# A two-layer hybrid backbone on one core: constant loads and a gate's modulation moved at the start, output chunks moved into the last attention stage

## The chip, the cores and the metric

One core of a Trainium2 chip runs the whole program. TensorE (PE) multiplies matrices out of SBUF into PSUM; its clock is granted at one of two levels, 1.2 and 2.4 GHz, which the profile gives as a share (0.50 and 1.00). VectorE (DVE), ScalarE (ACT) and GpSimd (POOL) do element-wise work; SyncE (SP) and ACT issue DMAs, each on a queue of its own (q1 is SP's, q10 is ACT's), and both queues feed the same 16 DMA engines. The metric is the device time of one execution in microseconds; the median of the timed runs counts, and less is better.

## The reference, cut to what matters

```python
D_MODEL, SEQ, CTX_LEN, DEPTH, D_FF = 1024, 512, 256, 2, 2816

for i in range(DEPTH):                      # layer 0: pooling mixer, layer 1: differential attention
    mod_l = (silu(c) @ ada_w[i] + ada_b[i]).reshape(9, D_MODEL)      # latent: shift, scale, gate for 3 sub-layers
    mod_c = (silu(c_ctx) @ ada_w[i] + ada_b[i]).reshape(9, D_MODEL)  # the same for the context tokens
    x = x + 0.5 * md[2] * swiglu(rms_norm(x) * g * (1 + md[1]) + md[0])          # first half step
    x = x + md[5] * mixer(rms_norm(x) * g * (1 + md[4]) + md[3])
    x = x + 0.5 * md[8] * swiglu(rms_norm(x) * g * (1 + md[7]) + md[6])          # second half step

# the attention of layer 1, for each of 8 heads
p = softmax(q @ k.T / 8)                    # twice, on two halves of the head
a = p[0] - lam * p[1]
o = rms_norm(a @ v, sub_g) * (1 - lam_init) # then o @ w_o, over all heads
```

Everything is float32. The 512 latent tokens and the 256 context tokens go through together; in layer 1 only the latent ones are kept after the attention.

## The kernel before, in words

Activations lie transposed: a tile holds 128 features by 768 tokens, and there are 8 such tiles. Every large product is taken in three passes on values split in a high and a low part (`h_hi`, `h_lo` and `w_hi`, `w_lo`): high times high, high times low, low times high. Per 128 output features (a *unit*; two units, `ch` 0 and 1, make a *pair*) ACT writes `w_hi` (L777), DVE writes `w_lo` (L1797), and PE multiplies (`chunk`, L1250, one chunk for one of the 8 feature tiles). The order on every engine is written out by hand in five programs, one for each engine, which meet in semaphores; nothing is scheduled by a tool. Each engine runs its instructions in that order, so whatever stands behind a waiting instruction waits too.

**The start.** SP issues the tokens (`xstage`), group 0 of the first modulation (`first_raw`, L526, 2 MB: shift and scale for two feature tiles, from `ada_w`), the weights of unit pair 0, and groups 1 to 3. ACT's queue brings the small tables, among them seven DMAs for constants that are used much later: `edge_sb` (pooling), `rope_sb`, four parts of `gqk` and `lam_sb` (attention), 576 KB in all. PE transposes the tokens (L1754), multiplies group 0 by silu(c) (`first_products`, L1492), spreads the inverse norm (L1482), multiplies group 1, and then alternates: the two feature tiles of a group through pair 0 for both `ch` (`first_pair`), then the products of the group after next. DVE turns a group's products into the modulation and makes `h_lo` (L2106).

**The modulation of the rest.** The first half step needs its gate (numbers 16 to 23 of the 72 blocks of 128 features) only where its first output pairs add to `x`. Two of these blocks come by a DMA of 1 MB (`gate_raw`, L564) and 32 small matmuls with two columns each (`gate_products`, L1504), which stand behind pair 1. The others come in *granules* of three blocks: SP loads 1.5 MB in two halves (`ada_raw`, L534), DVE multiplies and adds (L1814), ACT and POOL split the sum (L784, L790, L705), and two pairs later PE reduces it (`reduce_granule`, L1326, 18 matmuls with one column). One granule goes beside one pair of the FFN: 18 in the first FFN, beside pairs 1 to 18 of 30. The gate is made after pair 10 (`add_bias(0, GATE_FIRST, ...)`).

**The last attention stage.** The attention runs head by head; in stage `h` PE projects head `h`, scores head `h-1` over four tiles `s` of 128 queries (`score`, L1574), transposes its weights one tile behind (`turn_weights`, L1584), and head `h-2` gets its norm (`out_sums` L1611, `out_spread` L1622; DVE `out_norm` L2264). In the last stage (`h` = 8) nothing is left to project, and the product with `w_o` begins: `out_chunk(j)` is head `j`'s part of the first two output units, three matmuls of 512 columns for each `ch`, in bank `pv`. It needs ACT's `out_hi(j)` (L1138) and DVE's `out_lo(j)` (L2268). Chunks 0 and 1 stand in tile 0, chunk 2 behind the tiles, and chunks 3 to 7 after `values` (L1593, the product of weights and values), among the steps of the last head's norm. Then `unit` multiplies the other output pairs (bank `pu`).

## Time and profile before

| | us |
|---|---|
| three runs, median (lowest to highest) | 2584.11 (2583.5 to 2585.42) |
| the profiled execution | 2582.41 |
| its span (first to last instruction) | 2580.5 |
| PE busy | 2502.1 (97%) |
| DVE busy | 1564.8 (61%) |
| ACT busy | 872.6 (34%) |
| POOL busy | 427.4 (17%) |

A busy PE means that a matmul was in flight; at half the clock the same matmul is busy for longer, so the busy time says nothing of the clock. The granted clock is 0.98 over the whole span. All times of rows are from the span's start.

### The profile page before, as it was taken

What the parts mean: (1) busy time and instruction counts of PE and PEld (TensorE: products, weight loads), DVE (VectorE), ACT (ScalarE), POOL (GpSimd) and SP (SyncE); (2) the same over time, 40 slices, a digit from 0 to 9 for tenths busy, and PEclk for the clock granted to TensorE, in tenths of its full rate; (3) what the DMA queues carried; (4) which work ended last, traced back from release to release, by engine and by line L of the source; (5) the groups of instructions that cost most, each with busy time, mean ns of one, the idle gap of its engine ahead of it and who ended that gap; (6) DMA issues with size and microseconds to landing.
All of it is one profiled execution on the core that took longest, in us unless ns stands there. A gap on an engine that the chain in (4) does not pass through costs nothing.

```text
span 2580.5 us, 40749 instructions
## 1 busy us (share of the span) xinstructions
PE 2502.1 (97%) x14775; PEld 2217.2 (86%) x14775; DVE 1564.8 (61%) x2442; ACT 872.6 (34%) x1360; POOL 427.4 (17%) x517
## 2 busy tenths in 40 slices
PE   7999999999899999999999999999899988999999
PEld 7888888888788888888789999998789977788887
DVE  3788675224688857882584757574777774433332
ACT  2333132213533323331242423243455553322221
POOL 0121111001212111120100000001477751000000
PEclk9999999999899999999999999999899999899999
DMA  7555443221155534542122212222110111233332
GB/s 224 151 150 155 146 118 94 63 73 44 30 151 161 156 114 136 159 133 67 33 66 59 80 57 75 64 65 66 49 50 25 48 33 50 78 98 94 97 101 87
DMA packets 367021, 238.76 MB, mean 93 GB/s; under 512 B 7681, under 2 KB 365666, under 8 KB 366946
## 3 DMA queue, kind: packets, MB, share of 16 engines
q1 hardware_dynamic: 365104, 237.01, 31.4%
q10 hardware_dynamic: 1842, 0.77, 0.1%
q8 instruction: 45, 0.74, 0.1%
q14 instruction: 30, 0.25, 0.0%
HBM read 235.65 MB, written 2.10 MB: 92 GB/s over the span
## 4 chain that ended last, share of the span: by engine, by line
PE 91%; DVE 4%; ACT 2%; issue 1%; DMA 1%; POOL 1%; SPq 0%; ACTq 0%; DVEq 0%; POOLq 0%
PE pu L1250 63%; PE pu L1404 11%; PE pv L1556 5%; PE pu L1258 3%; PE pv L1492 1%; PE pu L1574 1%; PE pv L1584 1%; PE pu L1593 1%; DMA first_raw<-in_ada_w 1%; DVE h_lo L2106 1%; PE pv L1326 1%; DVE xn L2099 1%; PE pu L1529 1%; PE pu L1682 1%; DVE w_lo L1797 1%
## 5 line engine op out<-in xcount | busy, mean ns | idle before, releaser
L1250 PE MATMUL pu<-h_hi,w_hi 128*128 128x512 f32 (+1 forms) x1808 | 515.5, 350 | 3.4 <-DVE w_lo L1797 3.2
L1250 PE MATMUL pu<-h_hi,w_lo 128*128 128x512 f32 (+1 forms) x1808 | 513.5, 348 | 0.0
L1250 PE MATMUL pu<-h_lo,w_hi 128*128 128x512 f32 (+1 forms) x1808 | 513.2, 348 | 0.0
L1797 DVE TENSOR_TENSOR w_lo<-w_raw,w_hi 128x1024 fp32r<-128x1024 f32 (+3 forms) x228 | 311.3, 1366 | 249.8 <-ACT w_hi L777 242.3
L777 ACT ACTIVATE w_hi<-w_raw 128x1024 fp32r<-128x1024 f32 (+3 forms) x228 | 247.6, 1087 | 568.6 <-PE pu L1250 512.9
L1814 DVE SCALAR_TENSOR_TENSOR ada_acc<-ada_raw,cs,ada_acc 128x384 f32<-128x384 f32 x588 | 337.3, 616 | 10.7 <-DVE ada_acc L1814 1.8
L1250 PEld LDWEIGHTS pu<-h_hi,w_hi 128*128 128x128 f32 x1808 | 289.3, 188 | 50.7 <-DVE w_lo L1797 4.0
L1250 PEld LDWEIGHTS pu<-h_hi,w_lo 128*128 128x128 f32 x1808 | 289.9, 188 | 45.8
L1250 PEld LDWEIGHTS pu<-h_lo,w_hi 128*128 128x128 f32 x1808 | 289.0, 188 | 45.4
L2025 DVE SCALAR_TENSOR_TENSOR xT<-pu,gate,xT 128x512 f32 (+3 forms) x136 | 81.3, 634 | 332.1 <-PE pu L1250 329.0
L705 POOL TENSOR_TENSOR ada_acc<-ada_acc,ada_parts 128x768 f32<-128x768 f32 x84 | 142.3, 1694 | 726.8 <-ACT ada_parts L784 686.4
L1250 PE MATMUL pu<-a_hi,w_hi 128*128 128x512 f32 (+1 forms) x792 | 227.4, 350 | 0.6
L1250 PE MATMUL pu<-a_hi,w_lo 128*128 128x512 f32 (+1 forms) x792 | 226.4, 349 | 0.0
L1250 PE MATMUL pu<-a_lo,w_hi 128*128 128x512 f32 (+1 forms) x792 | 226.4, 349 | 0.0
L1250 PEld LDWEIGHTS pu<-a_hi,w_hi 128*128 128x128 f32 x792 | 127.2, 188 | 21.3 <-issue 0.4
L1250 PEld LDWEIGHTS pu<-a_hi,w_lo 128*128 128x128 f32 x792 | 127.1, 188 | 20.9
L1250 PEld LDWEIGHTS pu<-a_lo,w_hi 128*128 128x128 f32 x792 | 127.1, 188 | 20.8
L784 ACT ACTIVATE ada_parts<-ada_acc 128x768 bf16<-128x768 f32 x42 | 35.5, 845 | 322.0 <-PE pv L1326 310.2
L2011 DVE TENSOR_TENSOR prod<-pu,sil 128x512 f32<-128x512 f32 x116 | 63.3, 580 | 120.0 <-PE pu L1250 115.9
L801 ACT ACTIVATE sil<-pu 128x512 f32<-128x512 f32 x116 | 54.1, 508 | 222.7 <-PE pu L1250 222.7
L653 POOL TENSOR_TENSOR sqa<-sq 128x768 f32<-128x768 f32 (+2 forms) x6 | 9.1, 1517 | 666.4 <-ACT sq L822 659.5
L1556 PE MATMUL pv<-w_hi,h_hi 128*128 128x384 f32 (+1 forms) x336 | 112.4, 334 | 4.5 <-DVE w_lo L2254 4.5
(267 smaller groups left out, 4430.9 us busy)
## 6 DMA issues: line engine op xcount, KB each, us to landing
w_raw<-in_ffn_w_in SPq DMA_DIRECT2D x138, 512.0 KB, 3.9
ada_raw<-in_ada_w SPq DMA_DIRECT2D x84, 768.0 KB, 4.7
w_raw<-in_ffn_w_out SPq DMA_DIRECT2D x48, 704.0 KB, 4.6
w_raw<-in_ffn_w_in SPq DMA_DIRECT2D x76, 256.0 KB, 3.0
w_raw<-in_diff_w_qkv SPq DMA_DIRECT2D x24, 512.0 KB, 5.4
first_raw<-in_ada_w SPq DMA_DIRECT2D x8, 1024.0 KB, 12.2
w_raw<-in_ffn_w_out SPq DMA_DIRECT2D x16, 384.0 KB, 3.5
w_raw<-in_ffn_w_out SPq DMA_DIRECT2D x16, 320.0 KB, 3.2
```

The lines of the kernel that those rows point to most:

```text
L705: nc.gpsimd.tensor_tensor(rest, rest, ada_parts[:, i, :], ALU.subtract).then_inc(rest_ready, 1)
L777: act.activation(w_hi[:, ch, 0:k * P], w_raw[:, ch, 0:k * P], ACT.Copy).then_inc(hi_ready[ch], 1)
L784: act.activation(ada_parts[:, 0, :], ada_acc[:].rearrange("p s n -> p (s n)"), ACT.Copy).then_inc(part_ready, 1)
L801: i = act.activation(sil[:, SEG[s]], ps(0, s), ACT.Silu)
L1250: last = pe.matmul(banks(ch, s_), w[:, j, :], r[:, SEG[s_]], start=(j == 0 and i == 0), stop=(j == k - 1 and i == 2))
L1258: last = pe.matmul(tail_bank(i_, ch, s_), w[:, j, :], r[:, j, seg(i_, s_)], start=(j == 0 and i == 0), stop=(j == k - 1 and i == 2))
L1404: last = pe.matmul(pu[:, bank_of[p], 0:HN], w_[:, j, :], x_[:, j, :], start=(not adds and j == 0 and i == 0), stop=(j == HK - 1 and i == 2 ...
L1556: last = pe.matmul(pv[:, t % 2, at:3 * DV], x_[:, j, t * P:(t + 1) * P], aw[w_][:, j, at:], start=(j == 0 and i == 0), stop=(j == DC - 1 a ...
L1797: dve.tensor_tensor(w_lo[:, ch, 0:k * P], w_raw[:, ch, 0:k * P], w_hi[:, ch, 0:k * P].bitcast(F32), ALU.subtract).then_inc(split_ready[ch], 1)
L1814: last = dve.scalar_tensor_tensor(ada_acc[:, s_, :], ada_raw[:, b, i, :], w, ada_acc[:, s_, :], ALU.mult, ALU.add)
L2011: last = dve.tensor_tensor(prod[:, SEG[s]], ps(1, s), sil[:, SEG[s]], ALU.mult)
L2025: last = dve.scalar_tensor_tensor(xT[:, m, SEG[s]], banks(ch, s), gate[:, gk, s, m], xT[:, m, SEG[s]], ALU.mult, ALU.add)
```

## The change

It has three parts at the start and two in the last attention stage.

1. The seven constant DMAs go from ACT's program to SP's, behind group 3 of the first modulation.
2. `gate_raw`, its DMA and `gate_products` are gone. Granules begin one earlier (`ADA_FIRST` 5 for 6), so the first FFN has 19, beside pairs 1 to 19; the first of them holds blocks 15 to 17 (15 is computed once more and not used). Pair 1 on PE moves from a place of its own into the loop.
3. In `first_pair` the last group runs both its feature tiles for `ch` 0 and then both for `ch` 1, where before `ch` alternated within each tile.
4. Chunks 2, 3 and 4 stand behind the transposes of tiles 0, 1 and 2, chunk 5 where chunk 2 was, and the ACT and DVE parts that feed them move ahead accordingly. After `values` come chunk 6 for `ch` 0, the sums, the spread, chunk 7 for `ch` 0, then 6 and 7 for `ch` 1.
5. For the last head ACT squares straight from PSUM, before it copies to `oT`, where before it copied first and squared the copy. DVE's norm waits for that copy.

```diff
-ADA_FIRST = 2 * DC // ADA_CH + 1
+ADA_FIRST = 2 * DC // ADA_CH
-GATE_CH = ADA_CH * ADA_FIRST - GATE_FIRST
@@ SP
                         sp.wait_ge(h_ready[1], DC * (2 * n + 1))
-                        if n == 0:
-                            sp.dma_start(gate_raw[:], first[:, :, 2, 0:GATE_CH * P]).then_inc(gate_in, 16)
                         load_granule(n, 0)
...
             load_first(3)
+            sp.dma_start(edge_sb[:], edge.rearrange("g s e -> (g s e)").partition_broadcast(P)
+                          .rearrange("p (g s e) -> p g s e", g=len(WINDOWS), s=4)).then_inc(in_par2, 16)
+            sp.dma_start(rope_sb[:], rope.rearrange("t p a d -> p t a d")).then_inc(in_par2, 16)
+            for i in range(4):
+                sp.dma_start(gqk[:, i, :], qk_g[0, i // 2].partition_broadcast(P)).then_inc(in_par2, 16)
+            sp.dma_start(lam_sb[:], lam_p[0].rearrange("a d -> (a d)").partition_broadcast(P)
+                          .rearrange("p (a d) -> p a d", a=4)).then_inc(in_par2, 16)
             load_ffn(0)
@@ ACT, attn_act
+                if not do_a:
+                    out_hi(2)
                 for s in range(TT):
...
-                    if not do_a and s < QT:
-                        out_hi(s + 2)
+                    if not do_a and s < QT - 1:
+                        out_hi(s + 3)
...
                 if not do_a:
                     out_hi(HEADS - 2)
+                    act.wait_ge(pv_done, HEADS)
+                    act.wait_ge(ors_done, HEADS)
+                    act.activation(ob[:], pu[:, 0, :], ACT.Square).then_inc(osq_ready, 1)
@@ ACT, the seven constant loads go from here, and out_square(HEADS - 1) from behind attn_act(HEADS, ...)
...
@@ PE, ffn_pe
                             first_pair()
-                            for ch in range(2):
-                                unit(ch, 1, DC, lambda j: h_hi[:, j], lambda j: h_lo[:, j], n)
-                            gate_products()
-                            first = 2
+                        first = 1
@@ PE, first_pair
                 for g in range(GROUPS):
-                    for j in (2 * g, 2 * g + 1):
+                    js = (2 * g, 2 * g + 1)
+                    for j, ch in [(j, ch) for j in js for ch in range(2)] if g < GROUPS - 1 else [(j, ch) for ch in range(2) for j in js]:
@@ PE, attn_pe
                     if do_b and 1 <= s <= QT:
                         turn_weights(g, s - 1)
+                    if not do_a and 1 <= s < QT:
+                        out_chunk(s + 1)
...
-                    out_chunk(2)
+                    out_chunk(QT + 1)
                     out_spread(h - 2)
@@ PE, behind attn_pe(HEADS, ...)
-            out_chunk(3)
+            out_chunk(HEADS - 2, (0,))
             out_sums(HEADS - 1)
-            out_chunk(4)
             out_spread(HEADS - 1)
-            for j in range(5, HEADS):
-                out_chunk(j)
+            out_chunk(HEADS - 1, (0,))
+            for j in (HEADS - 2, HEADS - 1):
+                out_chunk(j, (1,))
@@ DVE, attn_dve
-                        out_lo(2)
+                        out_lo(QT + 1)
                     if do_b and 1 <= s <= QT:
                         weights_lo(g, s - 1)
+                    if not do_a and s < QT - 1:
+                        out_lo(s + 2)
                     if do_b and s < QT:
                         combine(step, g, s)
@@ DVE, behind attn_dve(HEADS, ...)
-            for j in range(3, HEADS - 1):
-                out_lo(j)
+            out_lo(HEADS - 2)
             out_var(HEADS - 1)
+            dve.wait_ge(oT_ready, HEADS + 1)
             out_norm(HEADS - 1)
```

What this makes of each engine's order, at three places (the third for PE and for ACT). Line numbers differ between the two kernels, since the change adds and removes lines.

SP's program at the start (the DMAs in the order in which they are issued), before:

```order
L526 DMA first_raw<-in_ada_w 128x8x256 [waits x_squares,xt_done]
L526 DMA first_raw<-in_ada_w 128x8x256 x3
L539 DMA w_raw<-in_ffn_w_in 128x8x128 [waits split_ready0]
L539 DMA w_raw<-in_ffn_w_in 128x8x128 [waits split_ready1]
L564 DMA gate_raw<-in_ada_w 128x8x256 [waits h_ready1]
L534 DMA ada_raw<-in_ada_w 128x4x384 [waits ada_half0]
L534 DMA ada_raw<-in_ada_w 128x4x384 [waits ada_half1]
```

and after:

```order
L520 DMA first_raw<-in_ada_w 128x8x256 [waits x_squares,xt_done]
L520 DMA first_raw<-in_ada_w 128x8x256 x3
L574 DMA edge_sb<-in_edge 128x128
L576 DMA rope_sb<-in_rope 128x4x128
L578 DMA gqk<-in_diff_qk_g 128x64 x4
L579 DMA lam_sb<-in_diff_lambda 128x256
L533 DMA w_raw<-in_ffn_w_in 128x8x128 [waits split_ready0]
L533 DMA w_raw<-in_ffn_w_in 128x8x128 [waits split_ready1]
L528 DMA ada_raw<-in_ada_w 128x4x384 [waits ada_half0,h_ready1]
L528 DMA ada_raw<-in_ada_w 128x4x384 [waits ada_half1]
```

The seven constant DMAs stand between group 3 and the weights of pair 1, and the gate's DMA is gone from behind them.

PE's program in the last attention stage, from the end of one tile's scores (`kT`, `qT`) over the transposes of the tile before (`ident,a`) to the next tile's scores, before:

```order
L1574 MATMUL pu<-kT_hi,qT_lo 128x384 x2
L1584 MATMUL pv<-ident,a 128x128 x6
L1574 MATMUL pu<-kT_hi,qT_hi 128x384 x2
L1574 MATMUL pu<-kT_lo,qT_hi 128x384 x2
L1574 MATMUL pu<-kT_hi,qT_lo 128x384 x2
```

and after (`h`, `w` are the operands of a chunk):

```order
L1557 MATMUL pu<-kT_hi,qT_lo 128x384 x2
L1567 MATMUL pv<-ident,a 128x128 x6
L1246 MATMUL pv<-h_hi,w_hi 128x512
L1246 MATMUL pv<-h_lo,w_hi 128x512
L1246 MATMUL pv<-h_hi,w_lo 128x512
L1246 MATMUL pv<-h_hi,w_hi 128x512
L1246 MATMUL pv<-h_lo,w_hi 128x512
L1246 MATMUL pv<-h_hi,w_lo 128x512
L1557 MATMUL pu<-kT_hi,qT_hi 128x384 x2
```

One chunk, six matmuls, has come between the transposes and the next scores.

PE's program behind the last head's `values`, from its sums of squares (`ones,ob`) on, before:

```order
L1611 MATMUL pu<-ones,ob 128x1 x4
L1250 MATMUL pv<-h_hi,w_hi 128x512
L1250 MATMUL pv<-h_lo,w_hi 128x512
L1250 MATMUL pv<-h_hi,w_lo 128x512
L1250 MATMUL pv<-h_hi,w_hi 128x512
L1250 MATMUL pv<-h_lo,w_hi 128x512
L1250 MATMUL pv<-h_hi,w_lo 128x512
L1622 MATMUL pu<-ident,orms 128x128 x4
L1250 MATMUL pv<-h_hi,w_hi 128x512
```

and after:

```order
L1594 MATMUL pu<-ones,ob 128x1 x4
L1605 MATMUL pu<-ident,orms 128x128 x4
L1246 MATMUL pv<-h_hi,w_hi 128x512
L1246 MATMUL pv<-h_lo,w_hi 128x512
L1246 MATMUL pv<-h_hi,w_lo 128x512
L1246 MATMUL pv<-h_hi,w_hi 128x512
```

No chunk stands between the sums and the spread any more. On ACT the square of the last head comes ahead of the copy; before:

```order
L1123 ACTIVATE aT_hi<-pv 128x3x128 [waits ta_done] x2
L1138 ACTIVATE h_hi<-oT 128x512 [waits on_ready]
L1170 ACTIVATE oT<-pu 128x512 [waits pv_done]
L1134 ACTIVATE ob<-oT 128x512 [waits ors_done,oT_ready]
L1138 ACTIVATE h_hi<-oT 128x512 [waits on_ready]
```

and after:

```order
L1122 ACTIVATE aT_hi<-pv 128x3x128 [waits ta_done] x2
L1137 ACTIVATE h_hi<-oT 128x512 [waits on_ready]
L1171 ACTIVATE ob<-pu 128x512 [waits ors_done,pv_done]
L1174 ACTIVATE oT<-pu 128x512 [waits pv_done]
L1137 ACTIVATE h_hi<-oT 128x512 [waits on_ready]
```

The square no longer waits for the copy, and the copy stands behind it.

## Rows read from the trace of the kernel before

**Rows 1.** The page: the chain that ended last, by engine.

```profile
PE 91%; DVE 4%; ACT 2%; issue 1%; DMA 1%; POOL 1%; SPq 0%; ACTq 0%; DVEq 0%; POOLq 0%
```

**Rows 2.** Waits of PE: who for whom, us in total, times, longest.

```profile
PE pu L1574 <- ACT e L1116: 11.0, 4, 4.3
```

**Rows 3.** Timeline of PE, first 131 us: start, us, instruction [idle before <-releaser].

```profile
24.53 8.71 PE L1492 MATMUL pv<-cs,first_raw 128*128 128x128 f32 x64 [3.10 <-DMA first_raw<-in_ada_w]
...
34.42 7.31 PE L1492 MATMUL pv<-cs,first_raw 128*128 128x128 f32 x64
...
57.05 7.31 PE L1492 MATMUL pv<-cs,first_raw 128*128 128x128 f32 x64
...
74.13 0.61 PE L1250 MATMUL pu<-h_hi,w_hi 128*128 128x512 f32 x2 [1.45 <-DVE w_lo L1797]
...
130.39 0.60 PE L1326 MATMUL pv<-ones_bf,ada_parts 128*128 128x1 bf16 x18
```

**Rows 4.** The chain of waits, first 100 us: start, us, what.

```profile
74.13 16.91 PE pu L1250 x96
91.05 3.47 PE pv L1504 x32
```

**Rows 5.** DMA queues from 8 to 24.5 us: packets, MB, share of 16 engines.

```profile
q10 hardware_dynamic: 1534, 0.64, 16.4%
```

**Rows 6.** DMA issues at 24.2 and 40 us (median us to landing); SP's timeline.

```profile
first_raw<-in_ada_w SPq DMA_DIRECT2D x2, 1024.0 KB, 9.6
...
40.04 3.39 SPq L539 DMA_DIRECT2D w_raw<-in_ffn_w_in  x1
...
w_raw<-in_ffn_w_in SPq DMA_DIRECT2D x1, 512.0 KB, 9.9
```

**Rows 7.** Timelines of DVE and ACT, first 110 us.

```profile
66.97 2.20 DVE L2106 SCALAR_TENSOR_TENSOR h_lo<-xn,mod,h_hi 128x512 fp32r<-128x512 f32 x4
...
71.76 1.06 ACT L777 ACTIVATE w_hi<-w_raw 128x1024 fp32r<-128x1024 f32 x1 [3.94 <-PE pu L1250]
```

**Rows 8.** Windows: us; busy of PE, PEld, DVE, ACT, POOL; PEclk, DMA, GB/s.

```profile
23.90:27.30 3.40, 2.77 (x13) 2.80 (x14) 0.00 (x0) 1.06 (x1) 0.00 (x0) 0.50 0.90 272
95.60:99.00 3.40, 3.40 (x12) 2.86 (x11) 3.12 (x6) 0.84 (x1) 0.05 (x1) 0.50 0.91 220
113.00:130.40 17.40, 17.35 (x109) 14.91 (x105) 15.09 (x21) 6.04 (x8) 3.33 (x2) 1.00 0.52 151
2119.70:2133.30 13.60, 8.30 (x40) 6.68 (x41) 11.07 (x22) 6.53 (x14) 0.00 (x0) 0.50 0.01 1
```

**Rows 9.** Timeline of PE in and behind the last attention stage.

```profile
2124.11 0.69 PE L1574 MATMUL pu<-kT_hi,qT_hi 64*128 64x384 f32 x2 [2.43 <-ACT e L1116]
...
2126.33 1.54 PE L1584 MATMUL pv<-ident,a 128*128 128x128 f32 x6
...
2149.39 1.05 PE L1611 MATMUL pu<-ones,ob 128*128 128x1 f32 x8
...
2151.78 1.16 PE L1622 MATMUL pu<-ident,orms 128*128 128x128 f32 x8
...
2158.82 0.50 PE L1250 MATMUL pu<-h_hi,w_hi 128*128 128x512 f32 x1 [1.79 <-DVE w_lo L1797]
```

**Rows 10.** The chain of waits in the same stretch.

```profile
2139.80 2.56 PE pv L1250 x6
2142.35 1.54 PE pu L1622 x8
...
2148.04 1.40 PE pv L1250 x6
```

**Rows 11.** Timelines of DVE and ACT in the same stretch.

```profile
2130.19 0.17 DVE L2242 RECIPROCAL rz<-zz 128x2 f32<-128x2 f32 x1 [0.59 <-ACT e L1116]
...
2154.42 0.69 DVE L2268 TENSOR_TENSOR h_lo<-oT,h_hi 128x512 fp32r<-128x512 f32 x1 [0.70 <-ACT h_hi L1138]
...
2148.70 0.63 ACT L1134 ACTIVATE ob<-oT 128x512 f32<-128x512 f32 x1
```

More of the change, by code:

```diff
@@ L1496, in first_products @@
                 last.then_inc(first_done, 1)
-            def gate_products():
-                pe.wait_ge(gate_in, 16)
-                for c_ in range(GATE_CH):
-                    at = 2 * (GATE_FIRST + c_)
-                    for j in range(DC):
-                        pe.matmul(pv[:, 2, at:at + 2], gate_raw[:, j, c_ * P:(c_ + 1) * P], cs[:, j::DC],
-                                  start=(j == 0), stop=(j == DC - 1))
             def first_pair():
@@ L1624, in out_spread, with out_chunk @@
                 last.then_inc(ors_done, 1)
-            def out_chunk(j):
+            def out_chunk(j, chs=(0, 1)):
                 if j == 0:
@@ L1632, in out_chunk @@
                 pe.wait_ge(on_split, j + 1)
-                for ch in range(2):
+                for ch in chs:
                     last = chunk(ch, j, DC, h_hi[:, j], h_lo[:, j], NL, wo_banks)
```

21 lines of the change are left out of this document (3 added, 18 removed).

## The prediction, made before the changed kernel was run

> **What bounds the kernel now.** I read the page's chain first: 91% of it is PE [rows 1], so the kernel is bound by PE's own matmuls, and only two kinds of thing can change the time by much: work that leaves PE, and the few places where PE waits or runs at 1.2 GHz. PE's waits are short and I looked for those at the change's places. At the start PE is free at 24.53 - 3.10 = 21.43 and waits 3.10 us for the DMA of group 0 [rows 3]. It waits 1.45 us for the split weights of pair 1 at 74.13 [rows 3]. In the attention it waits for ACT's exponentials, 11.0 us in 4 waits [rows 2], three of which lie in the last stage, the one shown 2.43 us long [rows 9]. Behind that stage it waits 1.79 us at 2158.82 for split weights [rows 9]. The windows show where the clock is at the lower of its two levels: 23.9 to 27.3 right after the 3.1 us wait, 95.6 to 99.0 right after the gate's small products, and 2119.7 to 2133.3 in the last attention stage [rows 8].
>
> **The constant loads.** From 8 to 24.5 us ACT's queue takes 16.4% of the 16 engines [rows 5], that is 0.164 x 16.5 = 2.7 us of all of them, and nearly all of its 0.64 MB is the seven moved DMAs (0.58 MB). Without them everything on SP's queue can land up to 2.7 us sooner: group 0 at about 21.8 and not 24.4. PE is free at 21.43, so its wait shrinks from 3.1 to some 0.4 us. The first products took 8.71 us, the later ones 7.31 [rows 3], and their first 3.4 us were at level 0.50 [rows 8]; with so short a wait I expect the full level, 1.4 us less. PE would be ready for group 1's products at 34.42 - 2.7 - 1.4 = 30.3. But group 1's second half is issued at about 24.2 and lands 9.6 us later, at 33.8 [rows 6], so this DMA comes next: 33.8 - 2.7 = 31.1. Start of the second products 34.42 -> 31.2: **-3.2**. From there the chain at the start is PE's own. Bounds: -1.5 (the queue keeps its own pace and only part of the share is returned, the clock still falls but for less) and -4.3 (PE itself is the limit: 34.42 - 30.1). The loads land later on SP's queue instead; pair 1's second weights are issued at 40.04 and landed at 49.9 [rows 6], ACT wants them at 71.76 [rows 7], so 2.7 us more there, and 3 us for seven issues, lie within 21 us of slack: 0.
>
> **The order in first_pair.** 96 matmuls take 16.91 us [rows 4], so two feature tiles for two units, 24 matmuls, take 4.2 and one tile for one unit 1.05. Before, unit 0 ended one such piece ahead of unit 1; now two. ACT's `w_hi` at 71.76 and DVE's `w_lo` behind it come 1.05 sooner, and PE's wait goes from 1.45 to 0.4: **-1.05**. What may take this back: tile 7 is needed sooner. Its `h_lo` ends at 66.97 + 2.20 = 69.17 [rows 7]; PE's last products start at 57.05 and take 7.1 of their 7.31 us before the next starts, two tiles follow (4.2), so PE comes to tile 7 of unit 0 at 68.3 + 1.05 = 69.4. That fits by 0.2. Bounds 0 and -1.45.
>
> **The gate.** The 32 small products go: **-3.5** [rows 4]. Pair 2's weights were split before they ended, so pair 2 follows at once. The stretch at level 0.50 behind them holds 12 matmuls in 3.4 us [rows 8] where full level gives twice as many: it cost about 1.6 us. I think the light products caused it, because dense pairs lie before and after and no wait: **-1.6**, bounds 0 and -1.7. One granule more is 18 matmuls on PE, **+0.6** [rows 3]. Beside a pair with a granule, DVE is busy 15.1 of 17.4 us, ACT 6.0 and POOL 3.3 [rows 8], so one more such pair is hidden on all three; it falls on pair 19, far from the end of that FFN at 30, and the gate still takes nine reduced granules by pair 10: 0. If DVE were not to fit, each microsecond over 17.4 would be one on PE. Dropping 1 MB from SP's queue ahead of granule 0 and adding 1.5 MB in the middle is hidden (DMA share 0.52 there).
>
> The Trainium skill (TensorE: Matmul & The Clock Gate, Part 1: The HAM clock gate) speaks against counting on the clock: it says that the slow stretch at the ramp varies from run to run with the same kernel, and that one should not fit to a count of slow matmuls. By that rule the terms for the clock would be left out and the start would give some 2 to 3 us less. The trace has both stretches only once, so it can't refute it.
>
> Start together: -3.2 - 1.05 - 3.5 - 1.6 + 0.6 = **-8.8**.
>
> **The tiles of the last stage.** A tile takes PE 2.2 us for scores (2124.11 to 2126.33), then the transposes [rows 9], then it waits about 2.4 us for the next exponentials. A chunk takes 1.40 us at full clock and 2.56 at half [rows 10]. So three of the four chunks go into waits that exist: at half clock they would overrun by 0.1 us at most. DVE waits 0.59 us for the exponentials [rows 11], and one `out_lo` (0.69) is put there: 0.1 us. What PE does more keeps it from light stretches, so the clock should come back earlier than 2133.3. Where it does, tiles shrink by a few tenths, and transposes, chunk and spread behind the last tile, which took 1.2 + 2.56 + 1.54 = 5.3 us at half clock [rows 9, 10], take 3.2. Bounds +0.4 (no better clock, small overruns) and -2.9. I take **-1.7**.
>
> **Behind the tiles.** Let V be the end of `values`, 2148.04 [rows 10]; the next unit starts at 2158.82, V+10.8. Now: ACT's square comes 0.63 sooner [rows 11], so the sums start at V+0.75 (2149.39 - 0.63). From sums to spread it took 2149.39 to 2151.78 [rows 9], 2.4 us, with a chunk as cover that is now gone: spread at V+3.15. From the spread's start to the end of the last `h_lo` it took 2151.78 to 2155.11 [rows 9, 11], 3.3 us: V+6.5. Chunk 7 of unit 0, half of 1.40: V+7.2. Then ACT's and DVE's split of the next weights, 2.4 us from ACT's start to PE's (71.76 to 74.13 [rows 3, 7], the same two steps): the unit starts at V+9.65, **-1.15**. But PE now idles 1.4 + 2.3 + 1.05 us of these 9.65, and the clock fell after stretches with such waits at 23.9 and at 2119.7 [rows 8]. Then spread and chunk are slower (1.54 for 1.0, 1.28 for 0.7 [rows 10]), which brings V+10.8 back, and the unit starts at half clock: 1.7 us lost if that goes on for as long as the shortest stretch of rows 8. Bounds -1.15 and +2.5. With some of both I take **0**.
>
> **Sum:** -8.8 - 1.7 + 0 = -10.5 us. It is made against the profiled execution (span 2580.5, time 2582.41), which lies 1.7 below the median of the three runs; taken to the median, 2584.1 - 10.5 = **2573.6**.
>
> **Rivals.**
> - *No head start.* Group 0 isn't held by the small loads but by SP's own 2 MB and the pace of its queue. For it: SP's own bytes before group 1 are ten times as many. Against: both share the engines and 16.4% is measured. Then 3.2 less of the gain: -7.3, 2576.8. The Trainium skill (DMA: Bandwidth & Descriptors, Issuing engines are not separate DMA queues) says that the engines interleave what any issuer started and that issuing from another one saves only the time to issue; by it the move of queue gives nothing, only the move behind the groups does. The trace agrees in that q10 took 16.4% of the engines beside SP's queue [rows 5].
> - *The tail gives it back.* The two bare waits behind the sums and the spread put the clock at half, the tiles gain nothing: -8.8 + 2.5 = -6.3, 2577.8. For it: the windows of 2119.7 to 2133.3. Against: chunks keep PE busier before it.
> - *Everything holds.* Group 1 doesn't bind (-4.3), all of the 1.45 goes, full clock in the tiles (-2.9) and behind (-1.15): about -13.7, 2570.4.
> - *Slower.* SP's program is in order and the weights of pair 1 and granule 0 now stand behind seven DMAs. If each had to land before the next is issued, at the 9.6 us of rows 6, 7 x 9.6 = 67 us would pass; from 21.8 us on (71.76 - 49.9) PE waits, so 45 us lost against 10.5 won: 2618. Against: SP was done with one issue in 3.39 us where its transfer took 9.9 to land [rows 6], so issues overlap.
>
> **Chances.** Forecast 0.55, no head start 0.17, tail gives back 0.15, everything holds 0.10, slower 0.03. A change of 0.2% (5.2 us) is about what the runs can tell from none. The first four are all beyond it, but both the second and the third together give -3.1, so I put 0.09 on within it: faster 0.88, same 0.09, slower 0.03. Range 2570.3 to 2578.3: it takes in both smaller gains and the full one, and leaves out their combination and the slower case.
>
> **What would show it.** The wait at the first group is under 1 us and the window behind it is at level 1.00; the second products start near 31; the wait for pair 1's weights is 0.4; no `gate_raw`, and no half-clock stretch near 90; PE's row for the granules has 774 matmuls for 756. In the last stage a chunk stands in each of three tiles with the wait for ACT shrunk by it; behind `values` two idle gaps of 1.4 and 2.3 us that name POOL or DVE. Wrong would be: a second group that lands at 33.8 as before, PE waiting for DVE beside pair 19, or a tile period that grows beyond 6.2 us (2124.11 to 2130.3).

## The result, and the profile after

The changed kernel takes 2570.57 us (median of 5 runs, 2568.22 to 2574.07), the kernel before 2584.33 in the same measurement (5 runs, 2583.5 to 2586.32). The ratio is 0.9941, 95% interval 0.9929 to 0.9953, that is 12.1 to 18.3 us less. A second measurement of both gave 2572.56 (5 runs) against 2586.92 (23 runs), ratio 0.994, interval 0.9927 to 0.9953. Forecast were 10.5 us less and 2573.6. The direction was right, the gain that was forecast was too small by 3 to 5 us. The median of 2570.57 lies at the lower edge of the stated range (2570.3 to 2578.3); the ratio, taken to the 2584.11 of before, gives 2568.9, which is below it.

The profiled execution took 2570.57 us with a span of 2568.8. PE is still the bound; the chain of the page now reads:

```profile
PE 90%; DVE 5%; ACT 2%; issue 2%; POOL 1%; DMA 1%; SPq 0%; ACTq 0%; DVEq 0%; POOLq 0%
```

**The start.** The timeline of PE in the changed kernel, to be held against [rows 3]:

```profile
20.30 7.31 PE L1484 MATMUL pv<-cs,first_raw 128*128 128x128 f32 x64
...
28.93 7.42 PE L1484 MATMUL pv<-cs,first_raw 128*128 128x128 f32 x64
...
67.71 0.62 PE L1246 MATMUL pu<-h_hi,w_hi 128*128 128x512 f32 x2 [0.41 <-DVE w_lo L1782]
...
101.74 0.60 PE L1322 MATMUL pv<-ones_bf,ada_parts 128*128 128x1 bf16 x18
```

The first products wait for nothing and run at full clock (7.31 us where they took 8.71); the second ones start at 28.93 and not at 34.42, 5.5 us sooner where 3.2 were forecast. The wait for pair 1's weights is 0.41 us, as forecast. The reduction of the first granule starts at 101.74; before, it started at 112.67. The chain of waits says what holds group 0. Before (start, us, what):

```profile
4.34 20.06 DMA first_raw<-in_ada_w
...
24.53 8.71 PE pv L1492 x64
```

and after:

```profile
3.44 8.70 DMA xstage<-in_ctx
...
19.37 0.87 PE pu L1739 x6
20.25 0.22 PE pv L1743 x2
20.46 7.15 PE pv L1484 x64
```

Before, the last link was the group's own DMA, 20 us long. Now the last DMA on the chain is the one of the context tokens, which lands at 12.1; from there PE's and DVE's transposes run without a gap. Group 0 itself is no longer on the chain. How long its two halves take from issue to landing, first before (the second half is issued at 4.34 and lands at 24.4) and then after (it is issued at 4.4 and lands at 18.2):

```profile
DMA to landing us min/median/max: 15.0/17.5/20.1
```

```profile
DMA to landing us min/median/max: 11.2/12.5/13.8
```

So group 0 lands 6.2 us sooner where 2.7 were forecast, ahead of the end of the transposes, and PE's own work sets the start of its products. The queues from 8 to 24.5 us, first before (packets, MB, mean rate; then the share of q1, SP's queue; q10 is in [rows 5]):

```profile
DMA packets 5451, 4.62 MB, mean 280 GB/s; under 512 B 765, under 2 KB 5180, under 8 KB 5451
...
q1 hardware_dynamic: 3917, 3.98, 73.5%
```

and after:

```profile
DMA packets 5914, 5.63 MB, mean 341 GB/s; under 512 B 172, under 2 KB 5638, under 8 KB 5914
...
q1 hardware_dynamic: 5771, 5.58, 108.9%
```

Taking 16.4% of the engines away from q10 gave q1 35 points more, and all queues together 61 GB/s more. The moved loads had cost more than the share that they took. The share adds up the times of the packets; since it can reach 108.9%, it isn't a part of a fixed 100% of which one queue gets what another leaves.

**The gate.** Behind pair 1 there is no half-clock stretch any more. Windows of the changed kernel (us; busy of PE, PEld, DVE, ACT, POOL; granted clock, DMA share, GB/s), against the second row of [rows 8]:

```profile
88.00:92.00 4.00, 4.00 (x25) 3.48 (x24) 3.76 (x5) 0.84 (x1) 1.43 (x1) 1.00 1.12 296
92.00:96.00 4.00, 4.00 (x25) 3.44 (x24) 3.37 (x6) 1.82 (x3) 0.00 (x0) 1.00 0.02 5
```

From pair 1 to the first reduced granule it takes 34.03 us, where it took 38.54.

**The last stage.** The timeline of PE, against [rows 9]:

```profile
2107.25 0.45 PE L1557 MATMUL pu<-kT_hi,qT_hi 64*128 64x384 f32 x2 [1.76 <-ACT e L1115]
...
2113.24 0.44 PE L1557 MATMUL pu<-kT_hi,qT_hi 64*128 64x384 f32 x2 [0.64 <-ACT e L1115]
...
2118.61 0.45 PE L1557 MATMUL pu<-kT_hi,qT_hi 64*128 64x384 f32 x2 [1.10 <-ACT e L1115]
...
2124.35 1.03 PE L1594 MATMUL pu<-ones,ob 128*128 128x1 f32 x8 [1.10 <-ACT e L1115]
...
2136.99 1.05 PE L1594 MATMUL pu<-ones,ob 128*128 128x1 f32 x8
2139.38 1.16 PE L1605 MATMUL pu<-ident,orms 128*128 128x128 f32 x8 [1.34 <-POOL orms L746]
...
2142.84 0.80 PE L1246 MATMUL pv<-h_hi,w_hi 128*128 128x512 f32 x1 [2.30 <-DVE h_lo L2253]
...
2146.95 0.50 PE L1246 MATMUL pu<-h_hi,w_hi 128*128 128x512 f32 x1 [0.46 <-DVE w_lo L1782]
```

The same waits in the kernel before, besides the one of 2.43 us at 2124.11 that [rows 9] show:

```profile
2118.12 0.44 PE L1574 MATMUL pu<-kT_hi,qT_hi 64*128 64x384 f32 x2 [1.78 <-ACT e L1116]
...
2130.30 0.69 PE L1574 MATMUL pu<-kT_hi,qT_hi 64*128 64x384 f32 x2 [2.44 <-ACT e L1116]
...
2136.24 1.36 PE L1611 MATMUL pu<-ones,ob 128*128 128x1 f32 x8 [2.46 <-ACT e L1116]
```

The three waits for ACT behind a chunk shrank from 2.4 us to 0.64, 1.10 and 1.10, and a tile takes 5.99, 5.37 and 5.74 us (2107.25 to 2113.24, 2118.61, 2124.35) where it took 5.99, 6.19 and 5.94 (2118.12 to 2124.11, 2130.30, 2136.24): 1.0 us less in all. Behind `values` stand the forecast waits that name POOL and DVE, 1.34 and 2.30 us. The clock of this stretch, against the last row of [rows 8]:

```profile
2108.20:2111.60 3.40, 2.94 (x14) 2.23 (x12) 3.30 (x6) 1.25 (x3) 0.00 (x0) 0.50 0.00 0
2111.60:2125.20 13.60, 9.01 (x61) 6.73 (x59) 12.81 (x27) 7.80 (x18) 0.00 (x0) 1.00 0.00 1
2125.20:2132.00 6.80, 5.82 (x23) 5.15 (x23) 2.95 (x6) 0.98 (x2) 1.39 (x1) 0.50 0.00 0
2132.00:2142.30 10.30, 7.20 (x38) 5.70 (x37) 2.56 (x5) 2.35 (x4) 1.01 (x1) 1.00 0.00 0
2142.30:2145.70 3.40, 2.86 (x7) 2.29 (x8) 1.26 (x3) 1.06 (x1) 0.00 (x0) 0.50 0.00 0
```

The half clock is there still, in three short pieces in place of long ones.

**What is compared below.** The time of one kernel drifts by several us from run to run (the kernel before: 2581.24 to 2594.49 in one measurement), so parts of 1 to 5 us are read from landmarks in the profiles: the start of the second products, pair 1, the first reduced granule, the spread ahead of the last attention stage (2109.25 before), the normalisation products behind the output projection (2191.12 before), and the end. A landmark belongs to one execution, so each is given as the mean over all the profiles that agree in that part, with their number. For the start, a second measure is how long the second half of group 0 takes from issue to landing: it doesn't depend on when PE is free.

### The profile page after: what moved, and what is told of

The parts are those of the page before. It is cut to its first block, busy times and chain, and to the rows that moved or that the text cites. A ratio compares the mean times of both kernels' runs of the same rounds, so it can differ in the third digit from the quotient of the medians.

```text
span 2568.8 us, 40790 instructions
## 1 busy us (share of the span) xinstructions
PE 2495.8 (97%) x14761; PEld 2209.3 (86%) x14761; DVE 1575.6 (61%) x2458; ACT 874.8 (34%) x1363; POOL 429.6 (17%) x519
## 4 chain that ended last, share of the span: by engine, by line
PE 90%; DVE 5%; ACT 2%; issue 2%; POOL 1%; DMA 1%; SPq 0%; ACTq 0%; DVEq 0%; POOLq 0%
PE pu L1246 63%; PE pu L1396 11%; PE pv L1539 5%; PE pu L1254 3%; PE pv L1484 1%; PE pv L1567 1%; PE pu L1557 1%; PE pu L1576 1%; DVE h_lo L2091 1%; PE pv L1322 1%; DVE xn L2084 1%; PE pu L1667 1%; PE pu L1512 1%; DVE w_lo L1782 1%; DVE mx L2212 1%
## 5 line engine op out<-in xcount | busy, mean ns | idle before, releaser
L1799 DVE SCALAR_TENSOR_TENSOR ada_acc<-ada_raw,cs,ada_acc 128x384 f32<-128x384 f32 x602 | 345.2, 615 | 11.0 <-DVE ada_acc L1799 1.8
```

Of the source, the lines that this page charges most:

```text
L1799: last = dve.scalar_tensor_tensor(ada_acc[:, s_, :], ada_raw[:, b, i, :], w, ada_acc[:, s_, :], ALU.mult, ALU.add)
```

## The experiments

### The loads alone

Before, with the seven loads behind `load_first(3)` on SP's queue:

```diff
             load_first(3)
+            sp.dma_start(edge_sb[:], ...)
+            sp.dma_start(rope_sb[:], ...)
+            for i in range(4):
+                sp.dma_start(gqk[:, i, :], ...)
+            sp.dma_start(lam_sb[:], ...)
...
-            act.dma_start(edge_sb[:], ...)
-            act.dma_start(rope_sb[:], ...)
-            for i in range(4):
-                act.dma_start(gqk[:, i, :], ...)
-            act.dma_start(lam_sb[:], ...)
```

> The kernel before with only the seven constant loads moved behind group 3 on SP's queue. Theory A (the loads alone set the start): PE begins group 0's products at 20.3 us without a wait for its DMA and group 1's at 28.9, where before had 24.5 and 34.4; 5.5 us less at that point, about 5.5 less in the time. Rival B (the forecast's size, the rest of the gain at the start comes from the other edits): group 1's products at about 31.2, 3.2 us less. Rival C (no head start): 34.4 as before, 0.

2581.3 us (10 runs) against 2587.12 (27 runs), ratio 0.9971, interval 0.9961 to 0.9981. PE in its profile:

```profile
20.77 7.32 PE L1492 MATMUL pv<-cs,first_raw 128*128 128x128 f32 x64
...
29.27 7.31 PE L1492 MATMUL pv<-cs,first_raw 128*128 128x128 f32 x64
```

29.27 lies among the 28.93 to 29.41 of the kernels with the whole change, so what is gained up to the second products is this edit's alone, and it explains the largest part of the surplus. The second half of group 0 lands 13.8 us behind its issue, as in the changed kernel. The time fell by 4.9 to 10.1 us, which agrees with the landmark but doesn't fix it.

### The gate alone

The gate's part of the change on the kernel before:

```diff
-ADA_FIRST = 2 * DC // ADA_CH + 1
+ADA_FIRST = 2 * DC // ADA_CH
...
-                        if n == 0:
-                            sp.dma_start(gate_raw[:], first[:, :, 2, 0:GATE_CH * P]).then_inc(gate_in, 16)
...
-                            for ch in range(2):
-                                unit(ch, 1, DC, lambda j: h_hi[:, j], lambda j: h_lo[:, j], n)
-                            gate_products()
-                            first = 2
+                        first = 1
```

> The kernel before with only the gate's two blocks made a granule. Expected if the light products caused the half-clock stretch behind them: the products go (-3.5), the stretch at 0.50 near 95.6 us goes too (-1.6), one more reduction (+0.6): -4.5. Rival (the stretch has another cause, or comes anyway): -2.9, and a stretch at 0.50 near 92 to 96 remains.

2579.91 us (10 runs), ratio 0.9972, interval 0.9961 to 0.9983. Pair 1 starts at 74.19 and the first reduction at 108.22:

```profile
74.19 0.62 PE L1242 MATMUL pu<-h_hi,w_hi 128*128 128x512 f32 x2 [1.45 <-DVE w_lo L1776]
...
108.22 0.60 PE L1318 MATMUL pv<-ones_bf,ada_parts 128*128 128x1 bf16 x18
```

That is 34.03 us apart, the same as in the changed kernel. The term holds by itself. The time fell by 4.4 to 10.1 us; the 4.5 expected lie at the lower end of that.

### The order of the first pair alone

```diff
-                    for j in (2 * g, 2 * g + 1):
+                    js = (2 * g, 2 * g + 1)
+                    for j, ch in [(j, ch) for j in js for ch in range(2)] if g < GROUPS - 1 else [(j, ch) for ch in range(2) for j in js]:
```

> The kernel before with only the last group of first_pair ordered unit by unit. Expected: PE's wait for pair 1's weights goes from 1.45 to 0.4 us, -1.05. Rival (tile 7's low part is needed too soon): a new wait for DVE's h_lo inside the last group takes it back, 0.

2587.19 us (10 runs), ratio 1.0, interval 0.999 to 1.0009. The wait is shorter by the forecast 1.04 us:

```profile
73.54 0.62 PE L1250 MATMUL pu<-h_hi,w_hi 128*128 128x512 f32 x2 [0.41 <-DVE w_lo L1797]
```

An effect of 1 us can't be seen in the time.

### The last stage alone, and the two kernels again

The edits of the last stage, all of them, on the kernel before; those of PE are:

```diff
+                    if not do_a and 1 <= s < QT:
+                        out_chunk(s + 1)
...
-                    out_chunk(2)
+                    out_chunk(QT + 1)
...
-            out_chunk(3)
+            out_chunk(HEADS - 2, (0,))
             out_sums(HEADS - 1)
-            out_chunk(4)
             out_spread(HEADS - 1)
-            for j in range(5, HEADS):
-                out_chunk(j)
+            out_chunk(HEADS - 1, (0,))
+            for j in (HEADS - 2, HEADS - 1):
+                out_chunk(j, (1,))
```

> The kernel before with only the edits of the last attention stage. Expected from the two profiles: the transposes of the last tile come 1.0 us sooner against the stage's start, and behind values nothing is won, so -1.0 in the stage. The forecast's size would be -1.7. Rival (the tail gives it back): +0.5 or more, with a long stretch at 0.50 behind values.

2579.56 us (5 runs), ratio 0.9966, interval 0.9952 to 0.9979: 8.8 us, against a forecast of 1.7 and a local difference of some 1 us between the first two profiles. One of the two had to be wrong, so it was run again, with both unchanged kernels beside it.

> The kernel before with the change of the last attention stage alone, a second time. Landmarks are the spread of the head before the last stage and the norm products that follow the output projection. In the profiles so far they are 81.9, 83.4, 83.2, 83.3, 81.9 and 82.2 us apart where the last stage is as before (mean 82.6), and 80.8, 78.9, 82.7 and 80.8 where it is changed (mean 80.8). Theory A, the landmarks are the whole effect and the 8.8 us of the first timing are drift of the clock between executions: the time is 1 to 3 us (0.04 to 0.12%) below that of the kernel before, ratio 0.9988 to 0.9996. Theory B, the changed stage is worth more in undisturbed executions than in profiled ones: the ratio is near 0.9966 again, and then the profiled execution is not above the timed ones.

2583.8 us (12 runs) against 2586.92 (23 runs), ratio 0.999, interval 0.9978 to 1.0001: 2.6 us, none to 5.7.

> The kernel before, unchanged, measured against itself as a scale for the other times: how far can two sets of runs of one kernel lie apart, and how does another profile of it differ. Theory A (drift of the clock between executions makes the sums of the parts too large): the ratio lies within 0.9990 to 1.0010, but its profile shows landmarks of the middle (first reduced granule to the spread ahead of the last stage) anywhere from 1995 to 2000 us, as in the eight profiles of kernels in which nothing was changed there. Theory B (the profile from which the forecast was made is not typical): its profiled execution is 2586 or more and its last stage has one unbroken half-clock stretch as in e1, e2 and e3.

2586.91 us (12 runs) against the same 23, ratio 0.9998, interval 0.9986 to 1.001. Its last stage has one unbroken half-clock stretch of 24 us, where the first profile of this kernel had two shorter ones:

```profile
2119.90:2143.80 23.90, 16.09 (x74) 13.03 (x72) 18.58 (x36) 10.86 (x24) 1.39 (x1) 0.51 0.00 1
```

> The changed kernel, unchanged, once more beside the same runs of the kernel before. By the profiles the change is worth 5.5 (loads) + 0.9 (order of the first pair) + 4.5 (gate) + 1.9 (last stage, means of the landmarks) = 12.8 us, so a ratio of 0.9950. By the first timing (0.9941) it is 15.2, by the sum of the four parts timed alone (7.5 + 7.2 + 0 + 8.8) 23.5 us, a ratio of 0.991. I expect 0.9942 to 0.9952.

2572.56 us (5 runs), ratio 0.994, interval 0.9927 to 0.9953.

Theory A of the two timings holds: the 8.8 us were a favourable set of five runs, and the interval over five runs didn't cover that. From the spread to the normalisation products, eleven profiles with the old stage take 81.9 to 83.4 us (mean 82.8), six with the new one 78.9 to 82.7 (mean 80.7; one of the six is the variant of the last experiment below, and without it the mean is 80.6): 2.2 us. The profile from which the forecast was made is, with 81.87, the shortest of its eleven. The middle, from the first reduced granule to the spread, isn't changed by the edits in a way that can be seen: 1993.8 to 2001.2 us over all profiles, 1997 us for the changed kernel once and 2001 the other time.

### Why the loads cost so much: their queue, or their time

The changed kernel, with the seven loads issued by ACT again, but there in the loop over the feature tiles, behind the first group's:

```diff
-            sp.dma_start(edge_sb[:], ...)
...
                 for s_ in range(2):
                     norm_hi(0, s_, j)
+                if j == 1:
+                    act.dma_start(edge_sb[:], ...)
+                    act.dma_start(rope_sb[:], ...)
+                    for i in range(4):
+                        act.dma_start(gqk[:, i, :], ...)
+                    act.dma_start(lam_sb[:], ...)
```

> The changed kernel with the seven loads back on ACT's queue, but behind ACT's norm of group 0 (about 31 us) where before they stood ahead of its first squares. Theory A (what counts is that they are behind the groups' transfers that PE waits for, not whose queue they are on): group 0's and group 1's products start at 20.3 and 28.9 as in the changed kernel, and the time is the same within 1 us. Rival (two queues at once slow SP's, wherever): group 2 or 3 or pair 1's weights come late, PE waits for a DMA, 1 us or more slower than the changed kernel.

2573.12 us (4 runs), ratio 0.9937, interval 0.9919 to 0.9955, too wide to tell 1 us. The loads are issued at 33.1 us, PE waits for none of the groups, and the second products start at 29.41. It is the time at which the loads are issued that counts; which engine issues them doesn't show.

### Which of the loads

First only the four `gqk` loads are moved (32 KB each), then only the other three (0.45 MB together); everything else as before:

```diff
             load_first(3)
+            for i in range(4):
+                sp.dma_start(gqk[:, i, :], ...)
...
-            for i in range(4):
-                act.dma_start(gqk[:, i, :], ...)
```

> The kernel before with only the four gqk loads moved (128 KB of the 576, but 512 of the 1280 packets). If the packets' number sets the loss: about 40% of the 5.5 us at group 1's products, 34.4 to 32.2. If the bytes do: a quarter or less, 33.2 or later.

2579.36 us (one run). PE in its profile:

```profile
21.45 7.39 PE L1492 MATMUL pv<-cs,first_raw 128*128 128x128 f32 x64
...
30.88 7.42 PE L1492 MATMUL pv<-cs,first_raw 128*128 128x128 f32 x64 [0.70 <-DMA first_raw<-in_ada_w]
```

> The kernel before with edge, rope and lam moved and the four gqk loads left on ACT's queue (448 KB, 768 packets). If packets: 60% of the 5.5 us, group 1's products at 31.1. If bytes: three quarters or more, at 30.2 or earlier.

2582.43 us (one run):

```profile
23.14 9.02 PE L1492 MATMUL pv<-cs,first_raw 128*128 128x128 f32 x64 [2.27 <-DMA first_raw<-in_ada_w]
...
33.83 7.41 PE L1492 MATMUL pv<-cs,first_raw 128*128 128x128 f32 x64 [0.33 <-DMA first_raw<-in_ada_w]
```

Against the mean of 35.1 of seven profiles with all the loads at the start, 0.13 MB are worth 4.2 us and 0.45 MB 1.3. At the landing of group 0 it is 3.4 and 1.7 us: its second half takes 16.9 us with `gqk` moved and 18.6 with the others moved, where the seven have a mean of 20.3. No price by bytes gives that, and a price by packets doesn't either (512 packets against some 810 in that stretch). Nor does a price by share. Where only `gqk` is left at the start, the queues from 8 to 24.5 us are:

```profile
q1 hardware_dynamic: 4456, 4.34, 83.2%
q10 hardware_dynamic: 701, 0.17, 4.6%
```

With the 1.2% that the small tables take in the changed kernel off, `gqk` has 3.4% of the 16.5 us, or 0.6 us; group 0 lands 4.8 us later than without any of the loads (18.6 against 13.8). A second execution of the first of them was taken later.

> The kernel of e6 (the loads of the q and k gains alone go to SP's queue behind the groups), a second execution. If its first was typical, group 0 waits for nothing and the second products start at 30.9 within 0.7; if it was chance, at 33 or more.

2580.21 us (one run); the second products start at 31.16, with a wait of 0.62 us ahead of group 0's, and group 0's second half lands after 17.0 us. The size was no chance.

### Small packets, or one row read by all

The four `gqk` loads read 256 bytes of DRAM for all 128 partitions. Here they read 128 different rows of 256 bytes:

```diff
-                act.dma_start(gqk[:, i, :], qk_g[0, i // 2].partition_broadcast(P)).then_inc(in_par2, 16)
+                act.dma_start(gqk[:, i, :], rope[i, :, 0, :]).then_inc(in_par2, 16)
```

> The kernel before, in which the four loads of the q and k gains take 128 different rows of 256 bytes each (from the rope table, so the gains are wrong) instead of one row for all partitions; queue, place, count and size of the packets as before. Start of the second products: 34.4, 36.8 or so in kernels with these loads at the start, 30.9 in e6 without them. Theory A, it is the small packets: 34 to 37 as before. Theory B, it is the one row that all partitions read: 30.5 to 31.5, as if these loads weren't there.

2580.26 us (one run). PE, and the queues from 8 to 24.5 us:

```profile
21.60 7.39 PE L1492 MATMUL pv<-cs,first_raw 128*128 128x128 f32 x64 [1.05 <-DMA first_raw<-in_ada_w]
...
31.37 7.42 PE L1492 MATMUL pv<-cs,first_raw 128*128 128x128 f32 x64 [1.04 <-DMA first_raw<-in_ada_w]
```

```profile
DMA packets 6346, 5.22 MB, mean 316 GB/s; under 512 B 776, under 2 KB 6081, under 8 KB 6346
...
q1 hardware_dynamic: 4811, 4.58, 90.1%
q10 hardware_dynamic: 1535, 0.64, 16.0%
```

Theory B holds. With as many small packets as before (776 under 512 bytes, 765 before), as many bytes and the same share for q10, the other queue goes from 73.5% to 90.1%, and the second products start 3.7 us ahead of the mean of the kernels with the broadcast (35.1). Not all of these 3.7 us are the transfer's: group 0's second half lands after 17.1 us and not 20.3, so 3.2 us sooner, the first products take 7.39 us and not 9.1 (their mean over the seven) at the better clock, and 1.0 us of this is lost again in a wait for group 1. What `gqk` costs goes away with rows of its own: 17.1 is what the two kernels without it at the start have (16.9, 17.0). The rows here also come from another tensor, and that part wasn't tested apart from their being different rows. Then the loads were doubled instead (the second set into a part of SBUF that isn't in use yet):

```diff
+            for i in range(4):
+                act.dma_start(sil[:, i * DH:(i + 1) * DH], qk_g[0, i // 2].partition_broadcast(P)).then_inc(spare_in, 16)
```

> The kernel before with the four loads of the q and k gains issued twice at the start (the second time into a part of SBUF that isn't used yet), 128 KB more. Theory A, their price is that of their packets (3.5 us for 512 of them): the second products start about 3.5 us later, at 38 to 40. Theory B, the price is not in their number but in that they share the engines at all: they start within 1 us of the kernel before, at 34.4 to 36.8.

2586.18 us (one run):

```profile
27.65 9.05 PE L1496 MATMUL pv<-cs,first_raw 128*128 128x128 f32 x64 [6.79 <-DMA first_raw<-in_ada_w]
...
37.88 7.31 PE L1496 MATMUL pv<-cs,first_raw 128*128 128x128 f32 x64
```

Here theory A's size holds and its reason doesn't: 512 more such packets cost 2.8 us over the mean of 35.1 (3.5 over the first profile of before, the figure from which the expectation was made), in line with the 3.7 of the first 512 (at the landing of group 0: 23.2 us against 20.3, so 2.9 for the second set and 3.2 for the first), but by e13 it isn't the price of small packets as such: with rows of their own, 512 of them cost next to nothing.

### Light products and the clock

Before, with 128 columns in each of the gate's products, where there were 2:

```diff
-                        pe.matmul(pv[:, 2, at:at + 2], gate_raw[:, j, c_ * P:(c_ + 1) * P], cs[:, j::DC],
+                        pe.matmul(pv[:, 3, c_ * P:(c_ + 1) * P].rearrange("p (n s) -> p n s", s=2),
+                                  gate_raw[:, j, c_ * P:(c_ + 1) * P],
+                                  cs[:, j::DC].unsqueeze(1).broadcast_to((P, P // 2, 2)),
```

> The kernel before, in which the 32 products for the gate have 128 columns of weights-side data moved through instead of 2 (results into a free part of the same PSUM bank, from which one VectorE operation takes the two that count), all else as before. It asks whether the light products are what brings the half clock behind the gate. From pair 1 to the first reduced granule it took 40.45, 40.43, 40.44, 38.5, 38.8 and 37.3 us with the light products, and 34.03 without the gate. Theory A, the light products cause it: they take about 3.5 us as before (their pace is that of the weight loads), no half-clock stretch follows, and the distance is about 37.5. Theory B, the clock there has another cause: a stretch at level 0.50 stands behind the gate again, with 38.5 to 40.5 us.

2584.85 us (one run):

```profile
91.38 3.74 PE L1503 MATMUL pv<-cs,gate_raw 128*128 128x128 f32 x32
...
111.91 0.60 PE L1326 MATMUL pv<-ones_bf,ada_parts 128*128 128x1 bf16 x18
```

Pair 1 started at 74.63, so the distance is 37.28, and no half-clock stretch stands there. That is as theory A has it, but it isn't shown by this: of eleven profiles with the light products two have none either, at 37.28 and 36.98 us. In the nine others the distance is 38.5 to 40.5. What is shown is that it comes only with the gate: none of the five profiles without the gate's products has it (33.4 to 34.0 us).

### Cover for the two waits behind the last head

The changed kernel, with chunk 5 between the sums and the spread, and one half of chunk 6 between the spread and chunk 7:

```diff
-                    out_chunk(QT + 1)
...
+            out_chunk(QT + 1)
             out_spread(HEADS - 1)
-            out_chunk(HEADS - 1, (0,))
-            for j in (HEADS - 2, HEADS - 1):
-                out_chunk(j, (1,))
+            out_chunk(HEADS - 2, (1,))
+            for ch in range(2):
+                out_chunk(HEADS - 1, (ch,))
```

> The changed kernel with chunk 5 taken from between the last tile's transposes and the spread, and put between the last head's sums and its spread, where PE idled 1.3 us; unit 1 of chunk 6 goes between the spread and chunk 7, where it idled 2.3 us. Theory (behind values PE waits for a fixed chain through ACT, DVE and POOL, and chunks there are free): values start 1.4 us (full clock) to 2.7 us (half) sooner less a wait of 0.4 for POOL, and the next unit stays at 10.8 us behind the end of values or comes at 9.7 if the clock holds: 1 to 3 us faster than the changed kernel. Rival (chunk 5 also covered POOL's orms for the spread before values): the wait there is 1.5 us or more and nothing is won.

2572.89 us (5 runs), ratio 0.9944, interval 0.993 to 0.9958, no difference from the changed kernel; the 1 to 3 us expected don't show, though an interval of 7 us can't rule out a gain of 1. In its profile the first wait is gone, the second is shorter, and a new one of 1.77 us for the next weights has taken their place:

```profile
2140.49 0.50 PE L1246 MATMUL pv<-h_hi,w_hi 128*128 128x512 f32 x1 [1.60 <-DVE h_lo L2253]
...
2143.92 0.49 PE L1246 MATMUL pu<-h_hi,w_hi 128*128 128x512 f32 x1 [1.77 <-DVE w_lo L1782]
```

From the last transposes to the next unit it takes 18.87 us (20.59 in the changed kernel), and from the spread to the normalisation products 80.77, within what the changed kernel shows by itself (80.82 and 79.28).

## Why the prediction was right in kind and too small

By its own steps, with the means over profiles:

| step | forecast | measured | profiles |
|---|---|---|---|
| loads, to the second products | -3.2 | -5.9 (35.1 to 29.2) | 7 and 5 |
| order of the first pair | -1.05 | -1.04 (wait 1.45 to 0.41) | e3 |
| gate and the clock behind it | -5.1 | -5.3 (39.2 to 33.9) | 11 and 5 |
| one more granule | +0.6 | not resolved | |
| last stage, to the normalisation | -1.7 | -2.2 (82.8 to 80.7) | 11 and 6 |
| sum | -10.5 | -13.8, with +0.6 as forecast | |

The sum of the measured terms is what the times show (13.8 by the medians of the first measurement, 14.4 by those of the second, 15.2 by the ratio). The added granule is there as forecast, 774 matmuls with one column for 756, but its 0.6 us can't be told in a middle that varies by 7.4 us.

**The step that failed is the price of the constant loads.** The prediction took q10's share of the engines, 16.4% of 16.5 us [rows 5], for the time that its loads cost the other queue, 2.7 us, and it set the full gain at 4.3 by PE's own work. Both were too small. In the seven profiles with all the loads at the start the second half of group 0 takes 19.8 to 20.9 us to land, in the five with none of them there 13.6 to 13.9: the loads cost the transfer 6.6 us. SP's own issues were held up as well. Those of pair 0's weights took 13.5 us and now take 7.7, so the second half of group 1 is issued at 18.0 and not at 24.2. It lands 10.9 us later, at 28.9, where the forecast had 31.1, and doesn't hold PE.

About half of the 6.6 us is what the four `gqk` loads cost by reading one row for all partitions: with rows of their own, which leaves the share at 16.0%, group 0 takes 17.1 us. What makes the other three loads cost from there to 13.8, some 3 us, stays open. `edge_sb` and `lam_sb` also read one row for all partitions (512 bytes and 1 KB), and no run gave them rows of their own. The share wasn't the price in either case: all seven loads have 15.2% and cost 6.6 us, where the share says 2.5; `gqk` alone has 3.4% and costs 4.8, where it says 0.6. With `gqk` on rows of its own the forecast's figures happen to be met (group 0's products at 21.60, the second ones at 31.37, forecast 21.8 and 31.2), but there all seven loads are still at the start: that agreement is luck.

No row of the share could show this, but one could have raised the question: all queues together moved 280 GB/s from 8 to 24.5 us, while SP's queue had work waiting, and 341 from 26 to 40 us. The 9.6 us that group 1 had to land [rows 6] are no such sign, since it takes 9.5 to 10.9 in the changed kernel too.

The bound of 4.3 rested on PE's being free at 21.43, which was late for this kernel: in the seven profiles PE is free at 20.9 on the mean, in the five at 20.6. (From [rows 3] the bound comes out at 34.42 - 3.10 - 1.40 = 29.9 and not 30.1, so 4.5 and not 4.3.) The rest of the way to 5.9 is that the second products of the profile used start at 34.42, where the mean is 35.1. So the likeliest case was mis-sized. The rival in which all holds named nearly the right sum for other reasons: group 1 doesn't bind, but the last stage gave 2.2 and not 4.05. Its terms also add up to -14.3 (-4.3 - 1.45 - 3.5 - 1.6 + 0.6 - 2.9 - 1.15) and not to -13.7, which is 2569.8, and that lies outside the range that was to take it in.

**No head start** is refuted by e1, and its half (only the position in time counts) is borne out: on ACT's queue, but later, the loads cost nothing (29.41). That agrees with what the Trainium skill states (DMA: Bandwidth & Descriptors, Issuing engines are not separate DMA queues).

**The clock.** The prediction counted 1.4 us at the first products and 1.6 behind the gate, against a page of the Trainium skill (TensorE: Matmul & The Clock Gate, Part 1: The HAM clock gate) that warns against it because slow stretches vary between runs. The runs bear out both. The stretches vary: behind a wait the same 64 first products take from 8.71 to 10.24 us, and behind the gate there are from none to 6.8 us at half clock. But none of the five profiles without the loads at the start and none of the five without the gate's products had one in that place, and the mean of the gate term is as forecast. At the first products it goes with the length of the wait: the three profiles in which it was 1.05 us or less while other loads were still there have none either, and all nine with 2.27 us or more have one.

**The last stage** came out as forecast in most of its parts: the chunks in the tiles shrink the waits, no tile grows, and from chunk 3 before or 6 after, the first one behind `values`, it takes 10.81 us to the next unit (10.94 before), the forecast 0, with the two waits where they were expected. One part did not come in the first profile of the changed kernel: the transposes, chunk and spread behind the last tile, which the forecast had at 3.2 us and full clock, took 5.5 us at level 0.50 (2126.36 to 2131.8). In its second profile they were at full clock. The stage's length varies with where the half clock falls: 78.9 to 82.7 us.

**Slower** was refuted at once: SP issues the seven loads in 7 us (31.8 to 38.9), and pair 1's weights wait for nothing new.

The profile of before also lay on the short side in three places: in its start (34.42, where seven such profiles have a mean of 35.1), behind the gate (38.54, mean 39.2) and in its tail (81.87, mean 82.8). These 2.3 us could not be read from that one execution, and they are chance. Held against that profile the terms are 5.2 for the loads, 1.0, 4.6 for the gate, -0.6 and 1.2 for the last stage, 11.4 in all where 10.5 were forecast: the loads gave 2.0 more than their term, the gate and the last stage 0.5 less each.

## What to carry to other kernels

A queue's share of the DMA engines isn't the price of its loads for the others: here it was 0.6 us for loads that cost 4.8, and 2.5 us for those that cost 6.6. If the sum over all queues falls below what the same kernel reaches elsewhere, while a queue has work waiting, look for loads in which all partitions read the same few hundred bytes, and issue them when nothing urgent is in flight. The time from issue to landing of the transfer that is waited for shows their price directly, where the start of the work behind it also holds the engine's own limits and its clock. A bound taken from when an engine was free holds only if what it did before didn't wait for the resource that is relieved. And a part of 0.1% is read from landmarks in several profiles, with the unchanged kernel among them, and not from the times of five runs.

## What was not expected of the hardware

Four loads of 32 KB that read one row of 256 bytes per load for 128 partitions held up the landing of a 1 MB transfer by 3.2 us (20.3 to 17.1 us from issue); the same loads with rows of their own held it up by nothing that can be told from not having them there (17.1 against 16.9 and 17.0). Twice as many held it up by 6.1 us against those (23.2). Whether it is the row in DRAM, the small tensor that it lies in, or something on its way that is asked for by all wasn't tried. A kernel measured against itself gave 0.9998 with an interval of 0.9986 to 1.001, but its single times lay 13 us apart.
